# Layer norms between projections: the sample tile first, the last tile in column halves

## The reference

```
x <- LN(a*x + mixer(x));  x <- LN(a*x + memory_cross_attention(x));  x <- LN(a*x + grouped_moe(x))

def post_norm(x, h, g, b):
    z = (DN_ALPHA * x + h).astype(F32)
    mu = jnp.mean(z, axis=-1, keepdims=True)
    var = jnp.mean(jnp.square(z - mu), axis=-1, keepdims=True)
    z = (z - mu) * lax.rsqrt(var + LN_EPS)
    return (z * g.astype(F32) + b.astype(F32)).astype(x.dtype)
```

## Time and profile before

| | us |
|---|---|
| median of 3 runs | 1433.52 (1432.91 to 1434.7) |
| the profiled execution's own time | 1435.86 |
| its span, first to last instruction | 1434.1 |
| granted TensorE clock, mean, share of full | 0.992 |

### The profile page before, as it was taken

How to read it: one execution, slowest core, us unless ns; L and a number is a source line. 1 busy time by engine, 2 the same in 40 slices (tenths; PEclk the granted TensorE clock), 3 DMA queues, 4 the chain that set the end, 5 groups by cost and what they waited for, 6 DMA issues and landing times.

```text
span 1434.1 us, 19792 instructions
## 1 busy us (share of the span) xinstructions
PE 1362.3 (95%) x7747; PEld 1138.9 (79%) x7747; DVE 1025.6 (72%) x1097; ACT 763.7 (53%) x788; POOL 120.1 (8%) x194
## 2 busy tenths in 40 slices
PE   6999999999889999999999999999889999999996
PEld 5879898779767788888887799778767788888884
DVE  4444766773547889888898365783548889898986
ACT  4343642432433677676777363332434677676775
POOL 6000045400000000000000014200000000000000
PEclk9999999999999999999999999999999999999998
DMA  8774454425884499899894346435883699898981
GB/s 262 248 233 151 145 177 144 133 91 176 315 331 177 169 335 348 330 337 331 333 343 171 117 151 206 129 118 176 347 323 124 230 336 343 326 348 324 337 335 37
DMA packets 99699, 343.72 MB, mean 240 GB/s; under 512 B 5984, under 2 KB 32112, under 8 KB 70432
## 3 DMA queue, kind: packets, MB, share of 16 engines
q1 hardware_dynamic: 96416, 331.90, 64.5%
q0 software_dynamic: 3200, 10.68, 2.3%
HBM read 327.61 MB, written 14.94 MB: 239 GB/s over the span
## 4 chain that ended last, share of the span: by engine, by line
PE 82%; DVE 11%; ACT 4%; issue 2%; DMA 1%; SPq 0%; DVEq 0%; ACTq 0%
PE ps L1733 64%; PE ps L2211 2%; PE ps L2066 2%; PE ps L2253 1%; PE ps L2088 1%; PE ps L2123 1%; PE ps L1742 1%; DVE mix_s L1460 1%; PE ps L2076 1%; PE ps L2153 1%; DVE x L1198 1%; PE ps L1741 1%; DVE x L1195 1%; PE ps L2202 1%; PE ps L1816 1%
## 5 line engine op out<-in xcount | busy, mean ns | idle before, releaser
L1733 PE MATMUL ps<-w_hi,xt_hi 128*128 128x512 f32 x704 | 280.1, 398 | 14.4 <-DVE w_lo L1131 7.8
L1733 PE MATMUL ps<-w_hi,xt_lo 128*128 128x512 f32 x704 | 276.1, 392 | 0.0
L1131 DVE TENSOR_TENSOR w_lo<-raw,w_hi 128x2048 fp32r<-128x2048 f32 x65 | 148.6, 2294 | 149.1 <-ACT w_hi L740 149.1
L1733 PE MATMUL ps<-w_lo,xt_hi 128*128 128x512 f32 x640 | 251.1, 392 | 0.0
L740 ACT ACTIVATE w_hi<-raw 128x2048 fp32r<-128x2048 f32 x65 | 123.8, 1913 | 163.7 <-PE ps L1733 92.8
L1135 DVE TENSOR_TENSOR moe_lo<-moe_in_raw,w_hi 128x2048 fp32r<-128x2048 f32 x72 | 164.3, 2291 | 29.5 <-ACT w_hi L747 29.3
L1135 DVE TENSOR_TENSOR w_lo<-raw,w_hi 128x2048 fp32r<-128x2048 f32 x72 | 164.9, 2292 | 25.3 <-ACT w_hi L747 24.0
L1733 PEld LDWEIGHTS ps<-w_hi,xt_hi 128*128 128x128 f32 x704 | 133.3, 189 | 45.6 <-issue 10.6
L747 ACT ACTIVATE w_hi<-moe_in_raw 128x2048 fp32r<-128x2048 f32 x72 | 138.1, 1918 | 51.0 <-PE ps L1733 51.0
L1733 PEld LDWEIGHTS ps<-w_hi,xt_lo 128*128 128x128 f32 x704 | 133.2, 189 | 28.6
L747 ACT ACTIVATE w_hi<-raw 128x2048 fp32r<-128x2048 f32 x72 | 137.5, 1912 | 12.0 <-PE ps L1733 12.0
(11 more groups left out here) (380 smaller groups left out, 2375.6 us busy)
## 6 DMA issues: line engine op xcount, KB each, us to landing
raw<-in_moe_w_gate SPq DMA_DIRECT2D x48, 1024.0 KB, 4.9
moe_in_raw<-in_moe_w_down SPq DMA_DIRECT2D x48, 1024.0 KB, 4.9
moe_in_raw<-in_moe_w_up SPq DMA_DIRECT2D x32, 1024.0 KB, 4.9
raw<-in_moe_w_up SPq DMA_DIRECT2D x32, 1024.0 KB, 4.9
raw<-in_xattn_w_kv SPq DMA_DIRECT2D x16, 1024.0 KB, 5.3
raw<-in_hgrn_w_in SPq DMA_DIRECT2D x16, 1024.0 KB, 5.7
raw<-in_cache_mem_k SPq DMA_DIRECT2D x16, 1024.0 KB, 4.9
moe_in_raw<-in_moe_w_gate SPq DMA_DIRECT2D x16, 1024.0 KB, 4.9
```

The lines of the kernel that those rows point to most:

```text
L1131: nc.vector.tensor_tensor(lo_at(slot_of(k)), raw_at(slot_of(k)), hi_at(hi_slot(k)).bitcast(F32), ALU.subtract).then_inc(w_low, 1)
L1733: ins = mm(out, lhs, rhs, start=start and n == 0, stop=stop and n == 2, skip_group_check=shared)
```

## The change

In the four norms between projections the order of tiles is 2, 0, 1 (`NORM_ORDER`) on all engines. TensorE makes the products of tiles 2 and 0, transposes tile 2, makes tile 1's products, transposes tile 0, runs 9 fillers and transposes tile 1 in two halves of four blocks with 3 fillers between them and 3 behind. VectorE normalises the last tile in two column halves of 512, each with its own semaphore (`ln_half` for the first, `ln_done` for the second), and then copies the first halves of tiles 0 and 1, then the second halves. The products behind (the query projection's first block and the router) wait for the three first copies ahead of row block 0, and for all five ahead of row block 4 (`rows_ready`). ScalarE follows the same order. The result banks of the transposes change with it, as does the router's bank. The wait numbers are renumbered by `nth` and `turns`; the norm behind the experts stays as it was.

```diff
+NORM_ORDER = (2, 0, 1)
+
+
+def nth(q, t):
+
+    return TILES * q + (NORM_ORDER.index(t) if q % 3 < 2 else t)
+
+
 def turns(u, t):
 
-    return 16 + 5 * (u - 2) + 2 * t
-
-
-def turn_bank0(u, t):
-
-    return (4, 6, 3)[t] if u == 4 else (0, 2, 7)[t]
+    return 16 + 5 * (u - 2) + (2 * t if u == 4 else (1, 3, 0)[t])
+
+
+def norm_bank(u, t, half):
+
+    return (4, 6, 3)[t] + half if u == 4 else ((6, 4), (5, 7), (7,))[t][half]
...
             def layer_norm(q, u, moe=False):
 
                 def rows_hi(t):
-                    act.wait_ge(ln_done, TILES * q + t + 1)
+                    act.wait_ge(ln_done, nth(q, t) + 1)
                     nc.scalar.activation(st_moe["xn_hi"][:, t, :], x[:, t, :], ACT.Copy).then_inc(mo[q // 3]["xh"], 1)
+                tile_rstd(q, 2)
+                turned(u, 2)
+                if moe:
+                    rows_hi(2)
                 tile_rstd(q, 0)
-                tile_rstd(q, 1)
-                if u:
-                    turned(u, 0)
                 if moe:
                     rows_hi(0)
-                tile_rstd(q, 2)
-                if u:
-                    turned(u, 1)
-                    turned(u, 2)
+                turned(u, 0)
+                tile_rstd(q, 1)
+                turned(u, 1)
                 if moe:
                     rows_hi(1)
-                    rows_hi(2)
...
-                xt = x[0:n, t, :]
-                link(nc.vector.scalar_tensor_tensor(out=xt, in0=xt, scalar=mean_var[0:n, t, 0:1], in1=ln_gb[0:n, 0, :],
-                                                    op0=ALU.subtract, op1=ALU.mult))
-                dve.wait_ge(ln_rstd, TILES * q + t + 1)
-                nc.vector.scalar_tensor_tensor(out=xt, in0=xt, scalar=rstd[0:n, t:t + 1], in1=ln_gb[0:n, 1, :],
-                                               op0=ALU.mult, op1=ALU.add).then_inc(ln_done, 1)
+                parts = ((0, NB), (NB, D)) if t == NORM_ORDER[-1] else ((0, D),)
+                for a0, a1 in parts:
+                    xt = x[0:n, t, a0:a1]
+                    link(nc.vector.scalar_tensor_tensor(out=xt, in0=xt, scalar=mean_var[0:n, t, 0:1], in1=ln_gb[0:n, 0, a0:a1],
+                                                        op0=ALU.subtract, op1=ALU.mult))
+                    dve.wait_ge(ln_rstd, nth(q, t) + 1)
+                    nc.vector.scalar_tensor_tensor(out=xt, in0=xt, scalar=rstd[0:n, t:t + 1], in1=ln_gb[0:n, 1, a0:a1],
+                                                   op0=ALU.mult, op1=ALU.add).then_inc(ln_done if a1 == D else ln_half, 1)
...
-            def turned(u, t):
+            def turned(u, t, halves=(0, 1)):
                 n = live(t)
                 per = NB // n
-                for half in range(KT // per):
+                for half in halves[0:KT // per]:
...
-                for t in range(TILES):
-                    if t < 2:
-                        dve.wait_ge(ln_tile, 2 * (q - q // 3) + t + 1)
+                for n, t in enumerate(NORM_ORDER):
+                    if n < 2:
+                        dve.wait_ge(ln_tile, 2 * (q - q // 3) + n + 1)
                     else:
+                        turned(u, 2)
                         dve.wait_ge(w_used, at(chunk_no(db) + 2, groups, GCH))
                     ins = add_tile(db, t, 1)
-                    if t == 2:
+                    if n == 2:
                         ins.then_inc(evac[par], 1)
                         dve.wait_ge(evac[par], db // 2 + 1)
                     else:
                         link(ins)
                     link(tile_stats(t, 1))
                     tile_norm(q, t)
-                    if t == 1:
-                        turned(u, 0)
-                turned(u, 1)
-                turned(u, 2)
+                turned(u, 0, (0,))
+                turned(u, 1, (0,))
+                turned(u, 0, (1,))
+                turned(u, 1, (1,))
...
-                for t in range(TILES):
-                    dve.wait_ge(s["xh"], t + 1)
+                for n, t in enumerate(NORM_ORDER):
+                    dve.wait_ge(s["xh"], n + 1)
...
+                        if u is not None:
+                            rows_ready(u, kt)
...
             def tile_block(db, groups, t):
 
                 par = db % 2
-                if t == 0:
+                if t == NORM_ORDER[0]:
                     pe.wait_ge(evac[par], db // 2)
                 for half in range(2):
                     k = chunk_no(db) + half
-                    if t == 0:
+                    if t == NORM_ORDER[0]:
                         pe.wait_ge(w_low, at(k + 1, groups, GCH))
                     r, rh = slot_of(k), hi_slot(k)
                     for kc in range(4):
                         kt = 4 * half + kc
                         ins = tile_products(par, r, rh, kc, kt, t)
-                if t < 2:
+                if t != NORM_ORDER[-1]:
                     ins.then_inc(ln_tile, 1)
                 else:
                     ins.then_inc(w_used, 2)
...
             def turn(q, u, t):
 
-                pe.wait_ge(ln_done, TILES * q + t + 1)
                 n = live(t)
                 per = NB // n
                 for kt in range(KT):
-                    ins = nc.tensor.transpose(ps[:, (0, 2, 7)[t] + kt // per, (kt % per) * n:(kt % per + 1) * n], x[0:n, t, kt * P:(kt + 1) * P], ident[0:n, 0:n])
+                    if t == NORM_ORDER[-1] and kt == 0:
+                        pe.wait_ge(ln_half, q - q // 3 + 1)
+                    elif kt == (4 if t == NORM_ORDER[-1] else 0):
+                        pe.wait_ge(ln_done, nth(q, t) + 1)
+                    ins = nc.tensor.transpose(ps[:, norm_bank(u, t, kt // per), (kt % per) * n:(kt % per + 1) * n], x[0:n, t, kt * P:(kt + 1) * P], ident[0:n, 0:n])
                     if kt % per == per - 1:
                         ins.then_inc(xt_ps, 1)
-                if t == 2:
-                    keep_busy(5, 5 if q % 3 < 2 else 4)
-                    pe.wait_ge(xt_l, turns(u, t) + 1)
+                    if t == NORM_ORDER[-1] and kt == 3:
+                        keep_busy(3, 0)
 
             def block_norm(db, groups, q, u):
+                tile_block(db, groups, 2)
                 tile_block(db, groups, 0)
+                turn(q, u, 2)
                 tile_block(db, groups, 1)
                 pe.wait_ge(evac[(db - 1) % 2], (db - 1) // 2 + 1)
-                if q % 3 == 0:
-                    keep_busy(9, 7)
                 turn(q, u, 0)
-                tile_block(db, groups, 2)
+                keep_busy(9, 0)
                 turn(q, u, 1)
-                keep_busy(18 if q % 3 == 0 else 20, 7)
-                turn(q, u, 2)
+                keep_busy(3, 0)
+
+            def rows_ready(u, kt):
+
+                if kt % 4 == 0:
+                    pe.wait_ge(xt_l, 16 + 5 * (u - 2) + (3 if kt == 0 else 5))
...
-                dense(db + 2, groups, "T")
+                dense(db + 2, groups, "T", u=2 + 3 * l)
...
-                    ins = three(ps[0:EXPERTS, 4, 0:TILES * P], r_hi[:, kt, :], r_lo[:, kt, :], xt_hi[:, kt, :], xt_lo[:, kt, :],
+                    rows_ready(3 + 3 * l, kt)
+                    ins = three(ps[0:EXPERTS, 0, 0:TILES * P], r_hi[:, kt, :], r_lo[:, kt, :], xt_hi[:, kt, :], xt_lo[:, kt, :],
```

More of the change, by code:

```diff
@@ L333, in decoder_step @@
         ln_tile = sem("ln_tile")
-        ln_mean = sem("ln_mean")
+        ln_mean, ln_half = sem("ln_mean"), sem("ln_half")
         ln_in, ln_var, ln_rstd, ln_done = sem("ln_in"), sem("ln_var"), sem("ln_rstd"), sem("ln_done")
@@ L771, in tile_rstd @@
             def tile_rstd(q, t):
-                act.wait_ge(ln_var, TILES * q + t + 1)
+                act.wait_ge(ln_var, nth(q, t) + 1)
                 rs = rstd[0:live(t), t:t + 1]
                 nc.scalar.activation(rs, rs, ACT.Ln).then_inc(act_step, 1)
-                act.wait_ge(act_step, TILES * q + t + 1)
+                act.wait_ge(act_step, nth(q, t) + 1)
                 nc.scalar.activation(rs, rs, ACT.Exp, scale=-0.5).then_inc(ln_rstd, 1)
@@ L797, in turned @@
                     nc.scalar.activation(xt_hi[:, per * half:per * (half + 1), t * P:t * P + n],
-                                         ps[:, turn_bank0(u, t) + half, :].rearrange("p (k s) -> p k s", s=n), ACT.Copy).then_inc(xt_h, 1)
+                                         ps[:, norm_bank(u, t, half), :].rearrange("p (k s) -> p k s", s=n), ACT.Copy).then_inc(xt_h, 1)
             def layer_norm(q, u, moe=False):
                 def rows_hi(t):
-                    act.wait_ge(ln_done, TILES * q + t + 1)
+                    act.wait_ge(ln_done, nth(q, t) + 1)
                     nc.scalar.activation(st_moe["xn_hi"][:, t, :], x[:, t, :], ACT.Copy).then_inc(mo[q // 3]["xh"], 1)
+                tile_rstd(q, 2)
+                turned(u, 2)
+                if moe:
+                    rows_hi(2)
                 tile_rstd(q, 0)
-                tile_rstd(q, 1)
-                if u:
-                    turned(u, 0)
                 if moe:
```

(25 more changed lines are left out.)

## The result

The changed kernel takes 1440.37 us (median of 5 runs, 1440.25 to 1440.96), the kernel before 1434.48 in its 5. The ratio is 1.0041, with a 95% interval of 1.0029 to 1.0053: slower by 5.9 us. The forecast was 1434.9 with a range up to 1438.3; it started from a median of 1433.52 for the kernel before, 1.0 us under the 1434.48 that stood beside the changed kernel.

The account below looks back on a forecast made before the run. TensorE was taken to bound the kernel, with the norm stretches set by VectorE. Mixer norms 2 x 0.2, clock 2 x 1.4 and attention norms -2 x 0.9 gave +1.4 us on median 1433.52: 1434.9, range 1431.2 to 1438.3.

Parts of the forecast that it names:

- The sign: Whole kernel: the change was forecast to make it slower, by +1.4 us.
- the price of the clock: Both mixer norms: half clock behind the new pause costs 1.4 us each, bounds 0.3 to 2.2.
- the start's row: Program start: 8 products in 3.3 us at half rate behind a 5.74 us pause, giving a price of 1.6 us.
- if a second one follows directly: Mixer norms: a second half-clock stretch gives up to 4.5 us at half rate, price 2.2 us.
- the sum: All four norms: 2 x 0.2 + 2 x 1.4 - 2 x 0.9 = +1.4 us.
- The pause: Mixer norms: TensorE stands 4.8 us ahead of the sample tile's transposes.
- Mixer norm without the clock: Norms behind the mixer: order and halves bring nothing, +0.2 us each, 26.1 us before the clock's loss.
- Behind attention: Norms behind attention: router's products 1.9 us earlier, score chain only 0.9, since VectorE's queue is last there.
- The slower one: Rival: the clock falls in all four norms, +6.2 us, 1439.7 us; chance 18%.
- The falls inside the norms behind attention: Part of the slower rival: pauses of 0.6, 0.4 and 0.2 us together bring a fall, 1.6 us each, 3.2 in all.
- No fall: Rival: the clock does not fall behind the new pauses, -1.4 us, 1432.1 us; chance 13%.
- 1.9 in all four: Rival: the halves bring their 1.9 us in all four norms, -7.6 us, 1425.9 us; chance 12%.

Follow-up runs that it names:

- e1: Changed kernel plus 20 filler products ahead of the sample tile's transposes in the two mixer norms: 1435.64 us, ratio 1.0006 to the kernel before.
- e5: On e2, VectorE subtracts the experts' first weight chunk behind the router's choice, not ahead of the score chain: 1430.20 us, ratio 0.9968 to the kernel before.
- e3: Changed kernel's tile order alone: last tile normalised and transposed whole, products behind wait for all five copies: 1442.51 us, ratio 1.0058 to the kernel before.
- e2_again: e2 measured again beside the two kernels that build on it: 1432.80 us, ratio 0.9992 to the kernel before.
- e2: Changed kernel with tile 1's products ahead of the sample tile's transposes in both mixer norms, 13 fillers ahead of tile 0's transposes: 1432.28 us, ratio 0.9989.
- e4: Changed kernel plus 9 filler products ahead of the sample tile's transposes in the two mixer norms: 1436.52 us, ratio 1.0015 to the kernel before.
- e6: On e2, 16 fillers instead of 12 between the router's transposes and the position products: 1431.83 us, ratio 0.9983 to the kernel before.

## Why the prediction was wrong

**Which step failed.** The sign was right and so were the large terms, but the price of the clock was mis-sized. "I take 1.4, near the start's row, less a little for the part that may pass in the pause": it measured 2.4 and 2.2 us a norm (28.94 and 28.71 against e1's 26.58 and 26.52), at and a little over the upper end of its own bounds, 2.2. I took the start of the program as the nearest row and read its 3.3 us at half rate as one whole stretch behind the pause. It was the tail of a longer one. The clock column of that row says 1.00 only because this trace has no clock record before 19.0 us; the half rate shows in its products. In e1's profile the records reach back, and the start's half clock holds 6.8 us, beginning 2.1 us before TensorE's return:

```profile
14.11:20.94 6.83, 4.73 (x11) 3.84 (x12) 3.38 (x2) 2.57 (x2) 5.89 (x16) 0.50 1.07 342
```

```profile
16.21 0.77 PE L1743 MATMUL ps<-w_hi,xt_hi 128*128 128x512 f32 x1 [6.20 <-DVE w_lo L1138]
```

Both mixer norms of the changed kernel are of the same kind:

```profile
316.02:322.85 6.83, 5.38 (x18) 4.39 (x19) 6.18 (x9) 1.01 (x3) 0.00 (x0) 0.50 0.00 1
957.73:964.55 6.82, 4.88 (x17) 3.99 (x18) 6.62 (x9) 1.00 (x3) 0.00 (x0) 0.50 0.00 0
```

The half clock spanned 6.8 us, began 1.5 and 1.9 us before TensorE resumed, and 5.4 and 4.9 were left for the work behind. I had this case as the bound "if a second one follows directly" and gave it no weight in the value; its own numbers (begun 2.1 us into a pause of 4.8) leave 3.9 us and a price of 1.95, not the 4.5 and 2.2 written there. The clock is 1.8 us of the 4.5 between the forecast difference (+1.4) and the measured one (+5.9).

**The rest of the miss.** With the right price of the clock the sum would have been +3.1. The mixer norms without the clock took 0.9 more than forecast for the two, the norms behind attention gave 0.6 less, and 1.3 stays open.

**Point by point.**
- VectorE takes the sample tile no earlier than it took tile 0 before the change: right (312.38 against 312.62 for a norm that starts 0.24 earlier). The pause: 4.75 and 4.69 us against 4.8.
- Mixer norm without the clock: forecast 26.1, e1 shows 26.5. A halved instruction takes 0.75 and not 0.69, which I had read from an add that reads accumulators, not from two tensors and a scalar in the same memory: splitting one costs 0.2, two 0.4.
- Behind attention: the router's products begin 1.4 us earlier, not 1.9; the score chain 0.6, not 0.9. That VectorE's queue gives the rest back was right, and e5 shows it. Together 0.6 us.
- Not in the sum: the pause of 1.15 us ahead of the position products, new because TensorE got ahead of VectorE. It costs 1.2 us (4.86 us from positions to gather in layer 0, 6.02 in layer 1) when the clock falls behind it.
- The Trainium skill's rule from "TensorE: Matmul & The Clock Gate", section "HAM oscillation", that the batch behind a long wait starts cold each time, was nearer than my value: by it I would have had 0.4 more, where the measured price is 1.8 more for the two. The traces agree with it for the four pauses of about 4.7 us (the changed kernel and e3), and not for one of 3.22 us in e2_again.

**The rivals.** The slower one had 18% and the closest time, 1439.7 for 1440.4. Of its parts the 2.2 in each mixer norm is what happened. The falls inside the norms behind attention, 3.2 of its 6.2, did not happen: the clock fell once, behind one of them. That its time came so close is luck. "No fall" is what e1 makes true by filler. "1.9 in all four" is out: even with VectorE kept busy (e2) a mixer norm gives 0.9 to 1.0, since its start stays bound by the add of the block before.

**What stays open.** Medians differ by 5.9 us and the traces account for 4.6 in the norms. The rest, 1.3, lies within what single stretches of half clock elsewhere add or remove from one kernel to the next, but no experiment isolates it. Nor is it shown what decides whether a pause is followed by half clock, in e4 or elsewhere.

## What to carry to other kernels

Before moving an instruction that waits ahead of work on an in-order queue, see whether what it waits for comes sooner too: here tile 1's products stood behind a wait that no earlier start had shortened. When filler work moves, count the pause that it leaves, and price a pause by the half clock that is left when work resumes, not by its length. And follow a gain to the next queue that is late: 1.4 us for TensorE was 0.6 for VectorE's chain until one instruction was moved behind it.

## What the runs showed of the hardware

**Whether the clock falls.** A pause of TensorE just over 2.6 us had two outcomes in one execution: behind 2.71 us twelve products ran at half rate, behind 2.65 us none. Length alone did not decide elsewhere either. The pause of 2.1 us that the earlier trace rows shows at 936.50 stands in all nine profiles, and half clock followed it in six. Behind this one in e2_again the clock stayed at 1.00:

```profile
108.94 1.51 PE L1871 MATMUL ps<-ident,x 128*128 128x128 f32 x12 [3.22 <-ACT kv_out L772]
```

```profile
104.00:120.00 16.00, 11.19 (x73) 9.66 (x72) 8.35 (x18) 6.85 (x13) 1.85 (x3) 1.00 0.59 190
```

All four pauses of about 4.7 us (the changed kernel and e3) had half clock; of the ten mixer norms in which filler or tile 1's products filled them (e1, e2, e2_again, e5, e6) none had.

**How long it holds.** The nine profiles hold 43 stretches of half clock apart from those at the very end. The 12 that began 0.7 us or more before TensorE's return held 6.8 us. The 31 that began later, all but one of them with TensorE already back, held 3.4. The long ones are not bound to long pauses; e4's stood at a pause of 2.71 us, e2's at one of 1.26 us:

```profile
317.77:324.60 6.83, 6.10 (x20) 4.92 (x21) 5.50 (x8) 1.00 (x3) 0.00 (x0) 0.50 0.00 1
```

```profile
418.64:425.47 6.83, 5.79 (x14) 4.43 (x15) 5.25 (x4) 3.79 (x3) 0.00 (x0) 0.50 0.69 263
```

So a shorter pause was not the cheaper one: behind e4's 2.71 us, 6.1 us of half clock met the work and cost 2.8 us; behind the changed kernel's 4.75 us it was 5.4, and 2.4.
